# Squares, low products and an early sum moved at the seams between matmul stages of a fused two-block network

## The reference

```python
h = h + 0.5 * rmsnorm_2(swiglu(rmsnorm_2(h, norm_g[0]), ffn1_gu, ffn1_down), norm_g[1])
z = rmsnorm_2(h, norm_g[2]) @ w_in        # ... three mixers on z -> mixed
h = h + rmsnorm_2(mixed, norm_g[3])       # mixed = concat @ w_out
h = h + 0.5 * rmsnorm_2(swiglu(rmsnorm_2(h, norm_g[4]), ffn2_gu, ffn2_down), norm_g[5])
gate = jax.nn.sigmoid(rmsnorm_2(h, norm_g[6]) @ ple_gate)
h = h + rmsnorm_2((p_i @ ple_proj) * gate, norm_g[7])
```

## Time and profile before

| | before |
| --- | --- |
| median of three runs | 2706.15 us |
| the profiled execution | 2708.01 us, its span 2706.2 us |
| granted TensorE clock, mean | 0.988 |
| PE, PEld busy | 2607.4 (96%), 2097.1 us |
| DVE, ACT, POOL busy | 1133.2 (42%), 997.6 (37%), 1261.9 us (47%) |
| chain that ended last | PE 85%, DVE 9%, issue 3%, ACT 2%, POOL 1%, DMA 1% |

### The profile page before, as it was taken

How to read it: one execution, slowest core, us unless ns; L and a number is a source line. 1 busy time by engine, 2 the same in 40 slices (tenths; PEclk the granted TensorE clock), 3 DMA queues, 4 the chain that set the end, 5 groups by cost and what they waited for, 6 DMA issues and landing times.

```text
span 2706.2 us, 33653 instructions
## 1 busy us (share of the span) xinstructions
PE 2607.4 (96%) x12436; PEld 2097.1 (77%) x12436; DVE 1133.2 (42%) x1712; ACT 997.6 (37%) x1482; POOL 1261.9 (47%) x1632
## 2 busy tenths in 40 slices
PE   6999999999999999999999999999999989999997
PEld 3788777787888877677888877888877767888875
DVE  5588666535221058625221046222018655222025
ACT  5233423524223244444323245323234454232234
POOL 1233467555555454135555455555544314555543
PEclk8999999999999999999999999999999999999999
DMA  6212211132333332112333322333322202333332
GB/s 269 70 55 71 79 46 40 54 118 86 101 95 94 100 92 67 35 56 85 96 99 93 102 93 80 100 94 96 99 86 84 63 24 86 93 95 100 95 96 74
DMA packets 63815, 234.24 MB, mean 87 GB/s; under 512 B 7361, under 2 KB 8001, under 8 KB 63169
## 3 DMA queue, kind: packets, MB, share of 16 engines
q1 hardware_dynamic: 61056, 222.33, 26.4%
q10 hardware_dynamic: 2624, 10.00, 1.0%
HBM read 230.00 MB, written 2.10 MB: 86 GB/s over the span
## 4 chain that ended last, share of the span: by engine, by line
PE 85%; DVE 9%; issue 3%; ACT 2%; POOL 1%; DMA 1%; SPq 0%; DVEq 0%; POOLq 0%; ACTq 0%
PE banks L1874 21%; PE banks L1864 21%; PE banks L1865 21%; PE banks L2215 2%; PE banks L2221 2%; PE banks L2216 2%; DVE tmp L1136 2%; DVE sq_sum L1115 1%; DVE xlo L1143 1%; PE banks L1934 1%; PE banks L2024 1%; PE banks L2336 1%; DVE h L1139 1%; PE banks L2285 1%; PE banks L2287 1%
## 5 line engine op out<-in xcount | busy, mean ns | idle before, releaser
L437 POOL TENSOR_TENSOR wlo<-raw,whi 128x256 fp32r<-128x256 f32 x1584 | 1181.8, 779 | 1371.9 <-ACT whi L528 1371.7
L1864 PE MATMUL banks<-xhi,whi 128*128 128x512 f32 x1920 | 752.5, 392 | 2.3 <-DVE z L1772 2.3
L1865 PE MATMUL banks<-xhi,wlo 128*128 128x512 f32 x1920 | 747.5, 389 | 0.0
L1874 PE MATMUL banks<-xlo,whi 128*128 128x512 f32 x1952 | 736.5, 393 | 10.2 <-DVE xlo L1143 10.1
L528 ACT ACTIVATE whi<-raw 128x1024 fp32r<-128x1024 f32 x396 | 415.1, 1053 | 348.3 <-PE banks L1874 337.8
L1874 PEld LDWEIGHTS banks<-xlo,whi 128*128 128x128 f32 x1952 | 365.8, 189 | 96.7 <-DVE xlo L1143 18.4
L1864 PEld LDWEIGHTS banks<-xhi,whi 128*128 128x128 f32 x1920 | 360.4, 188 | 82.0 <-DVE z L1772 3.1
L1865 PEld LDWEIGHTS banks<-xhi,wlo 128*128 128x128 f32 x1920 | 360.5, 188 | 76.5 <-issue 1.9
L1115 DVE TENSOR_TENSOR sq_sum<-sq_sum,tmp 128x512 f32<-128x512 f32 x110 | 85.3, 775 | 464.6 <-ACT tmp L548 464.6
L1864 PE MATMUL banks<-act_hi,whi 128*128 128x512 f32 x704 | 273.9, 389 | 0.0
L1865 PE MATMUL banks<-act_hi,wlo 128*128 128x512 f32 x704 | 273.9, 389 | 0.0
(11 more groups left out here) (419 smaller groups left out, 3186.8 us busy)
## 6 DMA issues: line engine op xcount, KB each, us to landing
raw<-in_stream SPq DMA_DIRECT2D x396, 512.0 KB, 3.5
ada_raw<-in_stream SPq DMA_DIRECT2D x24, 512.0 KB, 7.0
h<-in_x ACTq DMA_DIRECT2D x2, 2048.0 KB, 12.1
out<-h SPq DMA_DIRECT2D x4, 512.0 KB, 2.6
ctx_raw<-in_ctx ACTq DMA_DIRECT2D x1, 1024.0 KB, 19.6
...
ple_raw<-in_ple ACTq DMA_DIRECT2D x2, 512.0 KB, 3.5
...
```

Source lines behind the costliest of these rows:

```text
L437: piece = pool.tensor_tensor(wlo[:, i, s], raw[:, i, s], whi[:, i, s].bitcast(F32), ALU.subtract)
L1864: pe.matmul(acc[acc_of[t]][:], whi[:, u % SLOTS, i], x_h, start=(k == 0), stop=False, skip_group_check=split)
L1865: pe.matmul(acc[acc_of[t]][:], wlo[:, u % SLOTS, i], x_h, start=False, stop=False, skip_group_check=split)
L1874: mm = pe.matmul(acc[acc_of[t]][:], whi[:, u % SLOTS, i], x_l, start=False, stop=(k == k_tiles - 1), skip_group_check=leading and m < leads)
```

## The change

It moves instructions at the eight seams and adds none. In `norm_in` ScalarE's square of tile k - 3 follows the rounding of tile k (LAG = 4), and the last three squares follow the last rounding; unit 2 is cast ahead of tile 3 instead of tile 2, unit 3 still ahead of tile 5, and unit 4 ahead of tile 7, where before units 4 and 5 came behind the last square. In `boundary` VectorE adds the square of tile k - 4 behind x_low(k - 1), and the last four additions follow the last x_low. TensorE runs the low products of k - 1 behind the high products of k. The input norm's sum moves behind the leads: to the start of tile 5 (gu, gate) or amid tile 4 (in2, ahead of its fourth block). The output norm's early sum moves into the last output tile, two blocks ahead of its end (out1, down, out2); behind proj it stays behind the last product. At out1 VectorE's addition of tile 6's square moves ahead of the last residual.

```diff
@@ -39,6 +39,7 @@
 TURNED = 7
 LEADS = 4
 OUT1_LEADS = 2
+LAG = 4
 RING = (0, 1, 2, 3, 6, 7)
 RING_STAGES = ("gu", "down", "out2", "gate", "proj")
 UNIT = 8
@@ -560,10 +561,12 @@
 
                 high_parts(units_to(q) + SLOTS - 1)
                 for k in range(KT):
-                    if k == 2:
+                    if k == 3:
                         high_parts(units_to(q) + SLOTS)
                     if k == 5:
                         high_parts(units_to(q) + SLOTS + 1)
+                    if k == KT - 1:
+                        high_parts(units_to(q) + SLOTS + 2)
                     if k == 0:
                         for e in range(2):
                             s = slice(e * HALF, e * HALF + HALF)
@@ -576,6 +579,9 @@
                         act.wait_ge(*after("h_new", (q, k)))
                         act.activation(xhi[:, k], h[:, k], ACT.Copy, scale=gain[:, k:k + 1])\
                             .then_inc(*done("x_high", (q, k)))
+                    if k >= LAG - 1:
+                        squares("h_sq", q, k - LAG + 1, h[:, k - LAG + 1])
+                for k in range(KT - LAG + 1, KT):
                     squares("h_sq", q, k, h[:, k])
 
             def log_and_exp():
@@ -1143,7 +1149,10 @@
                         v.scalar_tensor_tensor(xlo[:, k - 1], h[:, k - 1], gain_pre[:, k - 1:k],
                                                xhi[:, k - 1].bitcast(F32), ALU.mult, ALU.subtract)\
                             .then_inc(*done("x_low", (q_pre, k - 1)))
-                        sq_add("h_sq", q_pre, k - 1)
+                        if k >= LAG:
+                            sq_add("h_sq", q_pre, k - LAG)
+                for k in range(KT + 1 - LAG, KT) if q_pre != "last" else []:
+                    sq_add("h_sq", q_pre, k)
 
             def mix_low(layer, t, src):
                 v.wait_ge(*after("mix_high", (layer, t)))
@@ -1533,10 +1542,12 @@
                 v.wait_ge(ld["x_again"], 16)
                 for m in range(KT):
                     t = first_tile["out1"] + m
+                    if m == KT - 1:
+                        sq_add("res_sq", "first", m - 1)
                     v.wait_ge(*after("product", ("out1", m)))
                     v.scalar_tensor_tensor(h[:, m], acc[acc_of[t]][:], mod[:, 2 * KT + m, 0:1], h[:, m], ALU.mult, ALU.add)\
                         .then_inc(*done("residual", m, bank_of=t))
-                    if m:
+                    if 0 < m < KT - 1:
                         sq_add("res_sq", "first", m - 1)
                     if m == 1:
                         prepare_angles()
...
+            def leading_high(stage, key, k):
+                for e, s in [(0, slice(0, HALF)), (1, slice(HALF, SEQ))] if k == 0 else [(1, slice(0, SEQ))]:
+                    for m in range(LEADS):
+                        t = first_tile[stage] + m
+                        if k == 0 and e == 0 and earlier[t] is not None:
+                            pe.wait_ge(*(bank_free(earlier[t]) or (ev.sem("product"), 1)))
+                        u, i = place(stage, m, k, KT, LEADS)
+                        if i == 0 or k == 0 and e == 0:
+                            pe.wait_ge(unit_split, u + 1 - WHOLE_UNITS)
+                        if m == 0:
+                            pe.wait_ge(*after("x_high", key(k) if k else (*key(k), e)))
+                        dst = acc[acc_of[t]][:, s]
+                        pe.matmul(dst, whi[:, u % SLOTS, i], xhi[:, k, s], start=(k == 0 and e == 0), stop=False, skip_group_check=True)
+                        pe.matmul(dst, wlo[:, u % SLOTS, i], xhi[:, k, s], start=False, stop=False, skip_group_check=True)
+            def leading_low(stage, key, k):
+                pe.wait_ge(*after("x_low", key(k)))
+                for m in range(LEADS):
+                    t = first_tile[stage] + m
+                    u, i = place(stage, m, k, KT, LEADS)
+                    mm = pe.matmul(acc[acc_of[t]][:], whi[:, u % SLOTS, i], xlo[:, k], start=False, stop=(k == KT - 1),
+                                   skip_group_check=True)
+                    keys = [("unit", u)] * (i == UNIT - 1) + [(stage, m)] * (k == KT - 1)
+                    if keys:
+                        mm.then_inc(*done("product", *keys))
+            def leading(stage, key):
+                for k in range(KT):
+                    leading_high(stage, key, k)
+                    if k:
+                        leading_low(stage, key, k - 1)
+                leading_low(stage, key, KT - 1)
...
-            def sum_squares(key, name, q):
-                if name == "h_sq":
-                    pe.wait_ge(*after("sq_added", (name, q, KT - 1)))
-                    pe.matmul(norm_bank[:], ones, sq_sum[:], start=True, stop=True).then_inc(*done("summed", key))
-                else:
-                    pe.wait_ge(*after("sq_added", (name, q, KT - 2)))
-                    halves = [slice(0, HALF), slice(HALF, SEQ)]
-                    for e, s in enumerate(halves):
-                        pe.matmul(bank[4 + e][:, 0:HALF], ones, sq_sum[:, s], start=True, stop=False)
-                    for e, s in enumerate(halves):
-                        pe.wait_ge(*after(name, (q, KT - 1, e)))
-                        pe.matmul(bank[4 + e][:, 0:HALF], ones, tmp[1 + (KT - 1) % 2][:, s], start=False, stop=True)\
-                            .then_inc(*done("summed", (key, e)))
+            def pre_sum(q):
+                pe.wait_ge(*after("sq_added", ("h_sq", q, KT - 1)))
+                pe.matmul(norm_bank[:], ones, sq_sum[:], start=True, stop=True).then_inc(*done("summed", ("pre", q)))
+            def first_squares(name, q):
+                pe.wait_ge(*after("sq_added", (name, q, KT - 2)))
+                for e, s in enumerate([slice(0, HALF), slice(HALF, SEQ)]):
+                    pe.matmul(bank[4 + e][:, 0:HALF], ones, sq_sum[:, s], start=True, stop=False, skip_group_check=True)
+            def last_squares(key, name, q):
+                for e, s in enumerate([slice(0, HALF), slice(HALF, SEQ)]):
+                    pe.wait_ge(*after(name, (q, KT - 1, e)))
+                    pe.matmul(bank[4 + e][:, 0:HALF], ones, tmp[1 + (KT - 1) % 2][:, s], start=False, stop=True, skip_group_check=True)\
+                        .then_inc(*done("summed", (key, e)))
...
@@ -2164,7 +2187,7 @@
                         after_tile=context_states)
                 ssd()
                 rest_of_out()
-                sum_squares("first", "res_sq", "first")
+                last_squares("first", "res_sq", "first")
 
             def rest_of_out():
 
@@ -2173,6 +2196,8 @@
                     if counted:
                         pe.wait_ge(*bank_free(earlier[t]))
                     for k in range(MIX_T):
+                        if (m, k) == (KT - 1, MIX_T - 2):
+                            first_squares("res_sq", "first")
                         u, i = place("out1", m, k, MIX_T, OUT1_LEADS)
                         if i == 0:
                             pe.wait_ge(unit_split, u + 1 - WHOLE_UNITS)
@@ -2417,19 +2442,30 @@
                 for s in range(4):
                     q = (layer, s)
                     tile = lambda k: (q, k)
-                    pre_sum = lambda: sum_squares(("pre", q), "h_sq", q)
+                    def sum_of_stream(at):
+                        return lambda m, k: pre_sum(q) if (m, k) == at else None
+                    def sum_of_output(k_tiles):
+                        return lambda m, k: first_squares("y_sq", q) if (m, k) == (KT - 1, k_tiles - 2) else None
                     if s in (0, 2):
-                        product(("gu", layer, s // 2), 2 * FT, KT, xhi, xlo, "x", tile, pre_sum, True)
-                        product(("down", layer, s // 2), KT, FT, act_hi, act_lo, "act", tile)
+                        gu, down = ("gu", layer, s // 2), ("down", layer, s // 2)
+                        leading(gu, tile)
+                        product(gu, 2 * FT, KT, xhi, xlo, "x", tile, LEADS, None, sum_of_stream((LEADS + 1, 0)))
+                        product(down, KT, FT, act_hi, act_lo, "act", tile, 0, None, sum_of_output(FT))
                     elif s == 1:
-                        product(("in2", layer), IN_T, KT, xhi, xlo, "x", tile, pre_sum, True,
-                                lambda m: m < IN_T - 1 and (hgrn_step(layer, m), gating_step(layer, m)))
+                        leading(("in2", layer), tile)
+                        product(("in2", layer), IN_T, KT, xhi, xlo, "x", tile, LEADS,
+                                lambda m: m < IN_T - 1 and (hgrn_step(layer, m), gating_step(layer, m)), sum_of_stream((LEADS, 3)))
                         attention(layer)
-                        product(("out2", layer), KT, KT, xhi, xlo, "mix", lambda k: (layer, k))
+                        product(("out2", layer), KT, KT, xhi, xlo, "mix", lambda k: (layer, k), 0, None, sum_of_output(KT))
                     else:
```

(6 more changed lines are left out.)

50 lines of the change are left out of this document (12 added, 38 removed).

## The result

The changed kernel takes 2717.14 us (median of 6 runs, 2715.89 to 2720.53) against 2707.18 of the kernel before, run beside it (6 runs, 2705.19 to 2709.90). The ratio is 1.0034, with a 95% interval of 1.0022 to 1.0045: slower by 6 to 12 us. Its profiled execution took 2716.39 us at a span of 2714.6, 8.4 over the span of before.

A forecast was written before the change was run, and what follows sets the result against it. TensorE was taken as busy 96% of the span, seven leads stretches held by VectorE. Terms summed to +6.55 us: profiled 2708.01 becomes about 2714.6; with the profile 1.86 over the median, the forecast is 2712.7, range 2703 to 2720.

The forecast's parts named there:

- (a): Leads of gu and gate: later squares and low products a tile behind gain 1.75 us in five stages, -8.75.
- (b): Output norm's early sum amid the last tile: +0.65 us in six down and out2 stages, +3.9; first seam -0.1.
- (c): in2, twice: later additions and clearing start z 2.15 us later, delaying tile 7, +4.3 in all.
- (d): Later input norm delays weight castings: stalls of 1.3 us in four gu stages (+5.2), 1.0 in gate twice (+2.0).
- GpSimd's third unit: Forming low parts of one more weight unit beside the boundary, said to stretch VectorE's steps by 2 us in all.
- T: Start of tile 4's first product in a stage; the forecast counts castings and tile starts from it.
- half clock now paid: Rival: gapless leads and new pauses make TensorE pay for 1.2 GHz stretches, up to 1.7 us each; 2721 to 2726, 12%.
- no new stall: Rival: weights come in time in gu and gate, the rest as forecast; 2705.5 us, 23%.
- the leads close wholly: Rival: TensorE reaches its gapless 22.85 us in five leads stages (-17.4), no stalls; 2694 us, 10%.

The follow-up runs named there:

- e6: Changed kernel with squares and additions back in the old order, low products still a tile behind: 2726.58 us, ratio 1.0071 to the kernel before.
- e5: Changed kernel without the early casting of unit 4, cast behind the last square again: 2748.57 us, ratio 1.0151 to the kernel before.
- e8: e7 with in2's squares, additions, low products, norm's sum and unit 4's casting as in the kernel before: 2701.69 us, ratio 0.9979.
- e10: The changed kernel once more, unedited: 2717.02 us, ratio 1.0034 to the kernel before.
- e2: Changed kernel with the input norm's sum amid tile 4 in gu and gate, instead of at tile 5's start: 2714.30 us, ratio 1.0024.
- e1: Changed kernel with the output norm's early sum back behind the last product at out1, down and out2: 2710.22 us, ratio 1.0011.
- e3: Changed kernel with in2's clearing of three buffers moved behind the first four z: 2716.74 us, ratio 1.0037 to the kernel before.
- e4: Kernel before with only the output norm's early sum moved amid the last tile at out1, down and out2: 2713.56 us, ratio 1.0027.
- e11: The kernel before once more, unedited, one run: 2707.52 us.
- e9: e8 with LAG = 6 and the input norm's sum ahead of tile 4's seventh block: 2699.40 us, ratio 0.9969 to the kernel before.
- e7: Changed kernel with the edits of e1, e2 and e3 together, early sum still amid out1's last tile: 2706.52 us, ratio 0.9992.

## Why the prediction was right

The forecast was 2712.7 and its range 2703 to 2720; the median is 2717.14, inside it and just above the forecast's own 2708 to 2717. Of the 4.4 between them, 1.0 is the base (2706.15 was taken, 2707.18 measured beside), 1.65 the sizes of the terms, and 1.8 stays open. The terms were the right ones, but in (a) the wait was the wrong one. They stand to the fixed differences between the traces like this:

| term | predicted | measured |
|---|---|---|
| (a) leads, 5 stages | -8.75 | 25.45 to 23.69: -1.75 each, -8.75 |
| (b) output norm's sum, 6 stages | +3.9 | +0.75 each, +4.5 |
| (b) first seam | -0.1 | 5.71 to 4.75, plus 0.86: -0.1 |
| (c) in2, twice | +4.3 | +2.58, +2.49: +5.1 |
| (d) gu, 4 stages | +5.2 | +1.3 each, +5.2 |
| (d) gate, twice | +2.0 | +1.06, +1.15: +2.2 |
| sum | +6.55 | +8.2 |

The stalls of (d) are what a stage lacks: a gu stage should be 1.75 shorter by (a) and 0.75 longer by (b); it is 0.30 longer, so 1.30 is stall. The starts of the tiles say the same (see (d) below).

- (a) The gapless first stage had only the sum to lose, and lost it. The five others gained 1.75, as forecast, but not in the way that was told. The step that the last low product waits for x_low(7) is wrong: before, x_low(7) was ready at 1001.50, while its products started at 1003.72, 2.2 later. What TensorE waited for last was x_low(5) then and is x_high(6) now (the two rows with 1.08 and 0.86). Three additions fewer stand ahead of these tiles as ahead of x_low(7) (there it is seven and four, not six and three), and e6 shows that the late squares matter. But a stretch of 23.7 that was worked out from a wait that doesn't occur, and then measured as 23.69, is in part luck.
- (b) was sized 0.1 too low per stage. The second sum does start 0.9 behind the last product, as I said, which is 0.22 earlier; but of that only 0.11 reaches the rounding. TensorE and ScalarE in the second seam, changed kernel:

```profile
974.77 0.40 PE L1859 MATMUL banks<-act_lo,whi 128*128 128x512 f32 x1
...
975.64 1.13 PE L1934 MATMUL banks<-tmp,table 128*128 128x256 f32 x4 [0.47 <-ACT tmp L547]
976.38 0.47 ACT L556 ACTIVATE inv_rms<-banks,small 128x256 f32<-128x256 f32 x1 [0.51 <-PE banks L1934]
```

  ScalarE's logarithm starts 0.74 behind the sum's start; before it was 0.63, with the sum running on out of the stream without a pause. The restart behind the new wait costs the 0.11 that I had left out.
- (c) was mis-sized most: 2.15 per stage against 2.5. The 2 us for GpSimd's third unit was right, since e5, without the unit, ends its last addition 2.05 earlier. What was too low is the price of the additions: I had taken 0.60 for each, which is the distance of VectorE steps that alternate, but in a row they start 0.80 apart (3.07 for four in e5). Three such distances make 0.6. TensorE's two waits between tiles 5 and 7, 2.71 and 1.38, are near the "some 5" of the forecast. The Trainium skill ("SBUF — State Buffer", Who interferes with whom) has VectorE steps with two SBUF inputs contend with GpSimd; the trace agrees with that and with its counterpart, since z, with an input in PSUM, takes 2.42 as before. By its rule (SBUF: two separate sides) that the loser blocks for the whole instruction the unit would cost up to 2.82; measured is 2.05, which is the rows' figure.
- (d) The train behind the late norm came as worked out: unit 6 of gu is cast at 1256.20, T + 7.75 (predicted T + 7.76), unit 8 at T + 19.8.

ScalarE in that stage, T = 1248.45, changed kernel:

```profile
1256.20 1.04 ACT L529 ACTIVATE whi<-raw 128x1024 fp32r<-128x1024 f32 x1
...
1268.22 1.99 ACT L529 ACTIVATE whi<-raw 128x1024 fp32r<-128x1024 f32 x2
```

  Tile 8 starts at T + 23.86, against T + 23.96. The stall is split, though. Tile 6, "just in time" in the forecast, starts at T + 12.30 instead of T + 11.76, 0.54 late. From there to tile 8 it is 1272.31 - 1260.75 = 11.56 instead of 10.88, 0.68 more, and tile 8 itself takes 0.12 more. The rows of the waits show only 0.35 and 0.40 of this 1.3, because they count from the end of the row before, which holds a tail (0.39, where products start 0.23 apart): 0.16 is missing from each, and behind each wait the first products lose another 0.12 or so.

What of the +9.96 between the medians the fixed terms leave, 1.8, is inside the comparison's interval (6 to 12 us). One part of it has a place: the first leads stage. It is gapless, so a stretch of 3.4 us at 1.2 GHz costs 1.56 there (e8: 365.86 against 364.30), one of 6.8 us 2.6 (e10). Such a stretch stands in seven of the traces with reordered leads (e2, e5 to e10), in three of them not (the changed kernel's, e1, e3), and in none of the three with the old order (before, e4, e11). It is the rival "half clock now paid", in one stage of the leads and not in five to eight. In the leads of gu and gate with LAG = 4 a single 3.4 us stretch costs next to nothing: 23.69 at granted clock 0.93 (changed kernel, above) and 23.68 at 1.00 (e8), because VectorE holds them. In those of in2 it costs up to 0.8 (24.53 in the sixth seam of e1), and 6.8 us cost 1.3 to 2.1 (25.03 in that of the changed kernel, 25.82 in e2's), of which at most 0.4 reaches z (30.31 in e2). In e9, whose leads have 0.6 of idle time left, the fifth stage's took 23.51 at 0.93 instead of 23.1. That a new pause can bring such a stretch and pay for it, as the rival has it, is shown by e5: a pause of 3.08, then 1.70 lost. The changed kernel's pauses of 0.35 to 0.66 bring none, but its new wait for z in in2 (2.3 to 2.7 us) does: a low stretch follows it in 11 of the 16 in2 stages that have this wait (changed kernel, e1 to e3, e5 to e7, e10), and stands in that place in none of the ten that don't. The wait ahead of tile 7 takes up most of it: with such a stretch it is gone, and tile 7 starts at 48.66 (changed kernel, sixth seam) as against 48.74 without (second seam, wait 1.38). That these stretches make the whole 1.8 is not shown.

Of the other rivals: "no new stall" fails by the waits for wlo and by e2, which removes them; "the leads close wholly" fails by 23.7 against the first stage's 21.96, since VectorE, busy for 23.3 to 23.4 of the stretch, remains the bound. The 10.1 us of waits for x_low did go, as it said, but waits for x_high took a part of their place.
